# Setup loads of the second layer moved ahead of a feed-forward's weights, one setup group one step earlier, and a new order in the gate of a hybrid decoder trunk

## What is computed

```python
for l in range(2):
    x = x + 0.5 * swiglu(rmsnorm(x, norm_ffn1[l]), ffn1_w_in[l], ffn1_w_out[l])
    z = rmsnorm(x, norm_mix[l]) @ mix_w_in[l]               # 1024 -> 3 x 512
    y_ssm = s5_group(z[..., :512], ...)                     # diagonal complex state space, 32 groups of 64 states
    y_gm = gmlp_group(z[..., 512:1024], z[..., 1024:], ...) # spatial gate
    y = concatenate([rmsnorm(y_ssm, gain_ssm_out[l]), rmsnorm(y_gm, gain_gm_out[l])])
    x = x + y @ mix_w_out[l]
    x = x + 0.5 * swiglu(rmsnorm(x, norm_ffn2[l]), ffn2_w_in[l], ffn2_w_out[l])
return rmsnorm(x, norm_final)

def gmlp_group(u, v, v_gain, w_s, b_s):
    u = gelu(u)
    v = gelu(v).reshape(1, 2, 128, 4, 128)                  # chunks of 128 tokens, 4 heads
    v = rmsnorm(v, v_gain.reshape(4, 128))
    s = einsum('hts,bnshd->bnthd', tril(w_s), v) + b_s      # causal product over the chunk's tokens
    return u * s
```

## Time and profile before

| | us |
|---|---|
| median of three runs | 938.13 (937.82 to 938.69) |
| the profiled execution | 938.69, its span 937.1 |
| TensorE busy | 927.1 (99%) |
| TensorE weight loads | 767.7 (82%) |
| DVE busy | 546.6 (58%) |
| ScalarE busy | 476.4 (51%) |
| GpSimd busy | 373.0 (40%) |
| DMA, mean | 176 GB/s, 165.08 MB |

### The profile page before, as it was taken

One profiled execution on the slowest core, in us unless ns is written; L12 is line 12 of the kernel. 1 busy time (PEld: TensorE's weight loads), 2 busy tenths in 40 slices (PEclk: granted clock), 3 DMA queues, 4 the chain that ended last, 5 costly groups with the idle time before them and its releaser, 6 DMA issues.

```text
span 937.1 us, 11925 instructions
## 1 busy us (share of the span) xinstructions
PE 927.1 (99%) x4582; PEld 767.7 (82%) x4582; DVE 546.6 (58%) x613; ACT 476.4 (51%) x687; POOL 373.0 (40%) x588
## 2 busy tenths in 40 slices
PE   9999999999999999999999999999999999999996
PEld 7888888888888888888888888888888888888885
DVE  4555655456976555664465555544688755555444
ACT  5544444456666444443464444434566654444432
POOL 5688998862513889998740000000033100000000
PEclk9999999999999999999999999999999999999999
DMA  8975555433256766555456555556524466656551
GB/s 239 244 240 181 180 180 182 177 135 135 91 181 202 202 183 183 179 193 200 145 154 203 181 180 180 180 197 205 167 104 137 133 202 192 190 181 204 182 175 45
DMA packets 129575, 165.08 MB, mean 176 GB/s; under 512 B 17640, under 2 KB 108912, under 8 KB 129520
## 3 DMA queue, kind: packets, MB, share of 16 engines
q1 hardware_dynamic: 129232, 163.80, 55.6%
q10 hardware_dynamic: 288, 0.53, 0.2%
HBM read 163.27 MB, written 1.05 MB: 175 GB/s over the span
## 4 chain that ended last, share of the span: by engine, by line
PE 97%; DMA 1%; SPq 1%; issue 0%; DVE 0%; ACT 0%; DVEq 0%; POOLq 0%; POOL 0%
PE bank L368 30%; PE bank L370 29%; PE bank L369 29%; PE bank L431 2%; PE bank L580 2%; PE bank L596 1%; PE bank L381 1%; PE bank L513 1%; PE bank L673 1%; DMA raw<-in_ffn_w_in 1%; PE bank L517 0%; PE bank L610 0%; SPq L256 0%; PE bank L627 0%; PE bank L637 0%
## 5 line engine op out<-in xcount | busy, mean ns | idle before, releaser
L960 DVE TENSOR_TENSOR w_lo<-raw,w_hi 128x1024 fp32r<-128x1024 f32 x303 | 381.8, 1263 | 311.4 <-ACT w_hi L742 311.4
L742 ACT ACTIVATE w_hi<-raw 128x1024 fp32r<-128x1024 f32 x303 | 320.3, 1061 | 309.1 <-PE bank L370 301.2
L368 PE MATMUL bank<-w_hi,x_hi 128*128 128x512 f32 x864 | 343.9, 398 | 0.2 <-DVE x_lo L975 0.2
L370 PE MATMUL bank<-w_hi,x_lo 128*128 128x512 f32 x864 | 337.3, 390 | 0.0
L369 PE MATMUL bank<-w_lo,x_hi 128*128 128x512 f32 x864 | 336.5, 389 | 0.0
L370 PEld LDWEIGHTS bank<-w_hi,x_lo 128*128 128x128 f32 x864 | 162.1, 188 | 35.0
L368 PEld LDWEIGHTS bank<-w_hi,x_hi 128*128 128x128 f32 x864 | 162.4, 188 | 32.3 <-DVE w_lo L960 0.6
L369 PEld LDWEIGHTS bank<-w_lo,x_hi 128*128 128x128 f32 x864 | 162.5, 188 | 31.8
L1186 POOL TENSOR_TENSOR rstd_c<-ms_c,neg_half 128x2 f32<-128x2 f32 (+1 forms) x8 | 5.3, 666 | 401.4 <-DVE ms_c L980 401.4
L368 PE MATMUL bank<-w_hi,h_hi 128*128 128x512 f32 x352 | 139.0, 395 | 0.0
L370 PE MATMUL bank<-w_hi,h_lo 128*128 128x512 f32 x352 | 137.2, 390 | 0.0
(11 more groups left out here) (151 smaller groups left out, 639.7 us busy)
## 6 DMA issues: line engine op xcount, KB each, us to landing
raw<-in_ffn_w_in SPq DMA_DIRECT2D x172, 512.0 KB
raw<-in_ffn_w_out SPq DMA_DIRECT2D x44, 1024.0 KB
raw<-in_mix_w_in SPq DMA_DIRECT2D x12, 1024.0 KB
raw<-in_mix_w_out SPq DMA_DIRECT2D x8, 1024.0 KB
raw<-in_ffn_w_in SPq DMA_DIRECT2D x8, 256.0 KB, 5.4
x<-in_x SPq DMA_DIRECT2D x6, 128.0 KB, 4.9
out<-x SPq DMA_DIRECT2D x6, 128.0 KB, 2.1
ws_raw<-in_gm_w_s SPq DMA_DIRECT2D x2, 256.0 KB
```

The costliest lines, as they stand in the source:

```text
L368: mm(o, hi_a, hi_b, start=first, stop=False)
L370: return mm(o, lo_a, hi_b, start=False, stop=last)
L742: A(w_hi[:, n % RING, :], raw[:, s, (n % 2) * 1024:(n % 2) * 1024 + 1024], ACT.Copy).then_inc(hi_done, 1)
L960: TT(w_lo[:, n % RING, :], raw[:, s, (n % 2) * 1024:(n % 2) * 1024 + 1024], w_hi[:, n % RING, :].bitcast(F32), ALU.subtract).then_inc(lo_d ...
```

## The change

Three parts of the program are written in another order; no arithmetic changes except that one power over 8 columns takes the place of two over 4.

1. The 19 setup transfers of layer 1 stood between the weights of blocks b = 1, 2 and 3 of layer 0's second feed-forward; now they stand together ahead of all its weights, behind the wait for `y_done`. Those of layer 0 stay.
2. GROUP_AT[0] is (9, 14, 16, 18) instead of (9, 14, 17, 18).
3. In `mix`, DVE splits half IN + 11 before it sums the squares; GpSimd runs `state(0)` before the gain products, and one power for both token halves after the first of them; ScalarE waits once for `vrs_done`.

```diff
@@ -39,7 +39,7 @@
 PREP = 8
 LOADS, LATE = 8, 3
 PREP_SMALL, PREP_C, PREP_WS = 1, 4, 8
-GROUP_AT = ((9, 14, 17, 18), (11, 14, 16, 18))
+GROUP_AT = ((9, 14, 16, 18), (11, 14, 16, 18))
 
 
 
@@ -273,16 +273,13 @@
                     for kk in range(2):
                         if p or b:
                             load_up(l, j, w_in, b, kk)
-                        if p < DEPTH and b == 1 and kk == 0:
-                            if p == 0:
-                                load_gains()
-                            else:
-                                sp.wait_ge(y_done, 2 * p)
-                            load_small(p)
-                    if p < DEPTH and b == 2:
-                        load_c(p)
-                    if p < DEPTH and b == 3:
-                        load_late(p)
+                        if p == 0 and b == 1 and kk == 0:
+                            load_gains()
+                            load_small(0)
+                    if p == 0 and b == 2:
+                        load_c(0)
+                    if p == 0 and b == 3:
+                        load_late(0)
                     if p < DEPTH and b in (5, 6):
                         load_gate(p, b - 5)
                 if p == 2 * DEPTH - 1:
@@ -349,6 +346,11 @@
                         load_in(l, j, kk)
                 for k in range(0, KT, 2):
                     load_rows(l, (OUT + k) // 2, a["mix_w_out"], (k + 4) % KT)
+                if l + 1 < DEPTH:
+                    sp.wait_ge(y_done, l * 2 + 2)
+                    load_small(l + 1)
+                    load_c(l + 1)
+                    load_late(l + 1)
                 load_ffn(l, 1)
 
             ov = out[0].rearrange("(h n j) d -> h j n d", j=T, n=32)
@@ -869,8 +871,8 @@
                 split(l, IN + 11)
                 split(l, OUT)
                 act.wait_ge(vss_done, l + 1)
+                act.wait_ge(vrs_done, l + 1)
                 for t in range(2):
-                    act.wait_ge(vrs_done, l * 2 + t + 1)
                     act.wait_ge(vgm_done, l * 2 + t + 1)
                     for i in range(HEADS):
                         w = slice(i * P, i * P + P)
@@ -1085,12 +1087,12 @@
                 scan(0)
                 split(l, IN + 10)
                 turn_out(0)
+                split(l, IN + 11)
                 dve.wait_ge(vsq_done, l + 1)
                 nc.vector.tensor_reduce(vss[:, :], vn[:].rearrange("p h (i d) -> p (h i) d", d=P), AXX,
                                         ALU.add).then_inc(vss_done, 1)
                 dve.wait_ge(vss_done, l + 1)
                 TS(vms[:, :], vss[:, :], 1.0 / P, EPS, ALU.mult, ALU.add).then_inc(vms_done, 1)
-                split(l, IN + 11)
                 scan(1)
                 turn_out(1)
                 dve.wait_ge(ug_done, l * 2 + 2)
@@ -1395,14 +1397,13 @@
                     pool.wait_ge(un_done, l * 8 + 4 * hf + 4)
                     nc.gpsimd.tensor_tensor(h_im[:, q, c], h_im[:, q, c], t3[:, q, :], ALU.add).then_inc(im_done, 1)
 
+                state(0)
                 pool.wait_ge(vsq_done, l + 1)
                 for t in range(2):
                     nc.gpsimd.tensor_tensor(vg[:, t, :], vg[:, t, :], vgain[:, :], ALU.mult).then_inc(vgm_done, 1)
-                pool.wait_ge(vms_done, l + 1)
-                for t in range(2):
-                    heads = slice(t * HEADS, t * HEADS + HEADS)
-                    inv_sqrt(vrs[:, heads], vms[:, heads], vrs_done)
-                state(0)
+                    if t == 0:
+                        pool.wait_ge(vms_done, l + 1)
+                        inv_sqrt(vrs[:, :], vms[:, :], vrs_done)
                 state(1)
                 pool.wait_ge(oms_done, l * 2 + 1)
                 inv_sqrt(ors[:, 0:2], oms[:, 0:2], ors_done)
```

## The result

The change is slower: 946.16 us in the median of four runs (945.07 to 949.99) against 937.98 for before (937.69 to 938.69), a ratio of 1.0089 with a 95% interval of 1.0065 to 1.0111. That is 8.2 us more, where 4.0 were forecast (942.1 against the 938.13 of the prediction), and above the range, which ended at 945.6. The profiled execution has a span of 944.0 us, 6.9 more than before's 937.1. Run a second time, beside other kernels, the same kernel took 944.12 against 937.72 (1.0065, 1.0049 to 1.0080). So the loss is between 6 and 8 us and differs between executions: all 33 executions of the changed kernel on record in the first comparison lie between 943.17 and 950.08 us, with a median of 946.07.

The account below looks back on a forecast made before the run. TensorE, 99% busy, was taken to bound the kernel. Stalls of 2.6 us (loads) and 1.4 us (group 2), with 0 in the gate, added 4.0 us to 938.13, giving 942.1 us, range 939.5 to 945.6.

Parts of the forecast that it names:

- The sum, term by term: Whole kernel: 2.6 us at the hand-over, 1.4 at group 2, 0 in the gate, together 4.0 us more.
- What bounds the kernel: Whole span: TensorE is 99% busy, waiting 2.3 us in all, so changes off it are free or cost time.
- Part 1, the wait named and the chain: Layer 0 hand-over: first ffn2_w_in block issued at 271.9 us, 4.2 us chain from split to residual, TensorE stops 2.6 us.
- Part 1, from issue to use: Layer 0 hand-over: ScalarE uses the first ffn2_w_in block 7.0 us after its issue; bounds 5.4 to 7.2.
- the opening's row: Kernel's opening: a weight block issued at 17.73 behind small loads was used at 24.95, 7.2 us later.
- The clock: Rival at the load stall: clock falls to half for four microseconds, costing 2 us, 944.1 us; chance 0.04.
- Part 2: Layer 0 setup group 2, near 188 us: TensorE waits 1.4 us for GpSimd's w1 copies; bounds 1.3 to 1.6.
- Part 3: the step that read the second power: Gate, both layers: the second power's 1.08 us beside a scan spoke against exclusion; 8-column power 1.7 us, loss 0.
- The rival itself: Gate: scan and power exclude each other, vn 1.5 us late in each layer, 945.1 us; chance 0.09.
- the block in time: Rival at the hand-over: first weight block comes in time, only part 2's 1.4 us left, 939.5 us; chance 0.13.
- w1 in time: Rival at layer 0 group 2: w1 is there in time, so no wait there, 940.7 us; chance 0.04.
- faster: Rival for the whole kernel: faster by over 0.2%, only if TensorE's pace itself changed; chance 0.02.

## Why the prediction was wrong

- **The sum, term by term.** In the profiled execution the rest cost 3.4 us where 2.6 were taken, group 2 1.2 instead of 1.4, the gate 0.8 instead of 0, and the clock 1.7 instead of 0; less 0.4 of the opening this is 6.7 against 4.0. The medians say 8.2 and 6.4, since the low stretch and the waits differ between executions.
- **What bounds the kernel: right.** TensorE had nothing to give, so the change could only cost.
- **Part 1, the wait named and the chain: right.** SyncE issued the first block at 273.06, the predicted 271.9 and the 1.2 us lost before. That the sum fits so well is luck, since single terms were off and met each other: small loads 5.6 us instead of 4.3, the B and gain loads 2.9 instead of 4.3. The C loads took the dear price, 5.1.
- **Part 1, from issue to use: too small.** 7.95 us where 7.0 was taken and 7.2 was the upper bound. The B pieces and the gain drained in front of the block (at most 6.1 us without them); the opening's row had no B pieces ahead of it and was not the bound it was used for. The rest was 3.4 us (2.6 to 3.4 in three executions) against 2.6 taken, with its bounds of 0 and 5.1.
- **The clock: the step that failed.** It was a rival with a chance of 0.04 and a price of 2 us, it stood in the sum with nothing, and in the range's upper end with nothing too. The reason given, that the engine rested for over 4 us at full clock at the tail, did not carry over: it fell with rests of 2.6, 3.0, 3.4 and 3.8 us in four profiled executions. One tail is one sample and no bound. The price was of the right size, 1.7 us in two of them and 3.0 in the others. The Trainium skill, page TensorE: Matmul & The Clock Gate, section HAM oscillation, tells of a kernel in which a wait on a transfer between dense products brought the clock down, so that the products after it started slow. The trace agrees with 0.50 after the rest, though here the transfer held TensorE only through DVE's order. That page spoke for a higher chance than 0.04.
- **Part 2: its place right, its bounds wrong.** 1.2 us in the change's profiled execution, and 1.3 to 2.1 in the medians, with waits of 1.2, 1.2, 2.1, 2.1 and 2.4 us in five profiled executions. The bounds of 1.3 to 1.6 came from one execution's GpSimd chain, whose arrival moves by 3.1 us against TensorE in the eight traces with the old place.
- **Part 3: the step that read the second power.** The power over 8 columns was put at 1.7 us beside the scans, and the gate at no loss. It took 2.48, 0.8 more, with 0.3 more in the second product (1.78 against 1.5); that is all of the 0.8 us of cover and 0.3 to 0.4 more. The argument had been that a power of 1.08 us ran over a scan. But the scan of 243.34 ended at 244.55, and that power began at 242.37 + 1.92 = 244.29: it had 0.26 us left to wait. The row did not speak against the page SBUF — State Buffer of the Trainium skill, section Who interferes with whom. The change's power fits a wait for the rest of the scan, 1.04 us, and 1.44 of its own, though alone it took 1.65; the scans that were issued into a running power and took 1.23 us do not fit an exclusion for the whole instruction. The rival itself was priced at 1.5 us in each layer, and 0.4 came: it let the power wait 1.2 us for one scan and the product as long for the other. The power took 0.8 more, and the product met no scan (the second ended at 247.42) but a DVE product of 0.69 us.
- **Rivals that did not come:** the block in time, which is what the kernel with `load_late` in its old place shows; w1 in time; faster.

## What to carry to other kernels

Where the bound engine has no idle time, price each wait that a change brings twice: the wait, and the clock behind it. Here waits of 2.6 us and more had the second price, those of 2.4 us and less had not, and a rest at the kernel's tail says nothing about one in the middle. Before small transfers are moved ahead of a large one, look at what stands in order behind the large one's first use; here one subtraction of DVE was enough, and moving DVE's splits, or leaving three of the 19 loads where they were, gave nearly all of the loss back. A slack of about 1 us behind GpSimd's long chain, read from one execution, is not a slack.

## What the runs showed of the hardware

- Rests of TensorE of 2.6, 3.0, 3.4 and 3.8 us came with a granted clock of 0.50. With 3.0 and 3.8 us it fell before the products resumed and stayed for 6.8 us; with 2.6 and 3.4 us it fell 1.3 and 1.0 us after they had resumed and stayed for 3.4 us. Rests of 1.2, 2.1 and 2.4 us left it at 1.00.
- At the tail of before the clock was at 1.00 for over 4 us after the last product.
- Two loads of 128 x 16 pieces of 64 bytes and one gain row took 2.9 us to issue and put at least 1.8 us on the time from the issue of the megabyte behind them to its use (7.95 against at most 6.1 us). From 273 to 277 us the DMA engines were 88% busy and more at 98 to 169 GB/s.
- A DVE scan takes 2.31 us instead of 1.21 beside a GpSimd product issued just before it, and 1.23 us when it is issued 1.14 us into a GpSimd power.
- GpSimd's power over 8 columns takes 1.65 us with DVE idle.
- GpSimd's setup chain of layer 0 reaches its copies of group 2 between 186.0 and 190.9 us in the profiled executions. Against TensorE, which shifts too, the spread is 3.1 us over the eight with the old group place and 1.2 us over the six with k = 16, and the copies themselves take 1.28, 2.16 or 2.35 us.
